# Third attention of a long two-block program: which PSUM banks hold scores and turned weights, and the order of TensorE's work in a step

## What is computed

```python
q = q.reshape(B, S, Hk, G, D) * (D ** -0.5)          # Hk=2 key/value heads, G=4 query heads each, D=64
...
s_c = einsum('bqhgd,bnhd->bhgqn', qc, kc) + head_bias(dist_c)      # compressed keys (31)
p_c = masked_softmax(s_c, dist_c >= 0)
...
s_s = einsum('bqhgd,bhqnkd->bhgqnk', qc, k_sel) + bias_s            # selected blocks of 64 keys
p_s = masked_softmax(s_s, mask_s)
...
s_w = einsum('bqhgd,bkhd->bhgqk', qc, kwc) + head_bias(dist_w)      # window of 512 keys
p_w = masked_softmax(s_w, mask_w)
...
return gc[..., 0:1] * o_c + gc[..., 1:2] * o_s + gc[..., 2:3] * o_w
```

## Time and profile before

| | us |
|---|---|
| median of 3 runs | 2223.79 (2222.8 to 2226.46) |
| the profiled execution, in all | 2226.47 |
| its span in the trace | 2224.7 |
| TensorE busy | 2183.1 (98%) |
| VectorE busy | 1276.9 (57%) |
| ScalarE busy | 945.7 (43%) |
| GpSimd busy | 804.4 (36%) |
| mean granted clock of TensorE | 0.994 |

### The profile page before, as it was taken

How to read it: one execution, slowest core, us unless ns; L and a number is a source line. 1 busy time by engine, 2 the same in 40 slices (tenths; PEclk the granted TensorE clock), 3 DMA queues, 4 the chain that set the end, 5 groups by cost and what they waited for, 6 DMA issues and landing times.

```text
span 2224.7 us, 25927 instructions
## 1 busy us (share of the span) xinstructions
PE 2183.1 (98%) x10008; PEld 1711.2 (77%) x10008; DVE 1276.9 (57%) x2198; ACT 945.7 (43%) x1558; POOL 804.4 (36%) x315
## 2 busy tenths in 40 slices
PE   8999999999999999999999999999999999999998
PEld 5777788888887767667888888887774688888887
DVE  6887665553258688773665562176967643333224
ACT  6676443333233566663344332233237532222224
POOL 1232444444443222113444444433330144444432
PEclk9999999999999999999999999999999999999999
DMA  8211333333222211112233333244310133233222
GB/s 281 67 58 53 93 95 98 102 95 104 95 93 78 72 48 39 39 33 90 96 99 95 95 105 103 90 125 165 112 60 11 38 95 95 95 99 109 91 100 85
DMA packets 58650, 199.97 MB, mean 90 GB/s; under 512 B 6720, under 2 KB 10320, under 8 KB 58528
## 3 DMA queue, kind: packets, MB, share of 16 engines
q1 hardware_dynamic: 57584, 196.21, 27.5%
q10 hardware_dynamic: 944, 2.11, 0.3%
HBM read 196.15 MB, written 7.38 MB: 91 GB/s over the span
## 4 chain that ended last, share of the span: by engine, by line
PE 88%; DVE 7%; ACT 2%; issue 1%; DMA 1%; POOL 0%; SPq 0%; DVEq 0%; ACTq 0%
PE lin L535 24%; PE lin L537 24%; PE lin L536 24%; PE obank L869 1%; PE scores L847 1%; PE turn L668 1%; PE scores L851 1%; PE stat L674 1%; PE scores L1070 1%; PE lin L586 1%; PE obank L748 1%; PE lin L588 1%; PE lin L587 1%; PE scores L705 1%; PE obank L1046 1%
## 5 line engine op out<-in xcount | busy, mean ns | idle before, releaser
L2540 POOL TENSOR_TENSOR w_lo<-slots,w_hi 128x1024 fp32r<-128x1024 f32 (+4 forms) x309 | 801.5, 2596 | 1395.9 <-ACT w_hi L2021 1395.9
L2021 ACT ACTIVATE w_hi<-slots 128x1024 fp32r<-128x1024 f32 (+4 forms) x312 | 347.0, 1113 | 576.9 <-DMA slots<-in_w_ffn_in 281.0
L535 PE MATMUL lin<-g_hi,w_hi 128*128 128x512 f32 x1400 | 550.0, 393 | 0.0
L537 PE MATMUL lin<-g_hi,w_lo 128*128 128x512 f32 x1400 | 545.0, 389 | 0.0
L536 PE MATMUL lin<-g_lo,w_hi 128*128 128x512 f32 x1400 | 544.9, 389 | 0.0
L535 PEld LDWEIGHTS lin<-g_hi,w_hi 128*128 128x128 f32 x1400 | 262.8, 188 | 59.3 <-issue 5.0
L536 PEld LDWEIGHTS lin<-g_lo,w_hi 128*128 128x128 f32 x1400 | 262.8, 188 | 55.8 <-issue 1.7
L537 PEld LDWEIGHTS lin<-g_hi,w_lo 128*128 128x128 f32 x1400 | 262.7, 188 | 54.7
L1255 DVE TENSOR_TENSOR h<-lin,h 128x512 f32<-128x512 f32 x72 | 49.7, 690 | 306.1 <-PE lin L537 296.9
L536 PE MATMUL lin<-f_lo,w_hi 128*128 128x512 f32 x528 | 205.4, 389 | 0.0
L535 PE MATMUL lin<-f_hi,w_hi 128*128 128x512 f32 x528 | 205.4, 389 | 0.0
(11 more groups left out here) (479 smaller groups left out, 3526.9 us busy)
## 6 DMA issues: line engine op xcount, KB each, us to landing
slots<-in_w_ffn_in SPq DMA_DIRECT2D x132, 512.0 KB, 3.5
slots<-in_w_ffn_out SPq DMA_DIRECT2D x48, 704.0 KB, 4.0
slots<-in_w_ple SPq DMA_DIRECT2D x24, 640.0 KB, 3.8
slots<-in_w_a_qkv SPq DMA_DIRECT2D x24, 512.0 KB, 3.6
slots<-in_w_c_in SPq DMA_DIRECT2D x21, 512.0 KB, 3.6
slots<-in_w_b_wo SPq DMA_DIRECT2D x16, 512.0 KB, 3.5
slots<-in_w_b_pair SPq DMA_DIRECT2D x8, 768.0 KB, 4.2
slots<-in_w_a_wo SPq DMA_DIRECT2D x16, 256.0 KB, 2.6
```

Source lines behind the costliest of these rows:

```text
L535: pe.matmul(bank[:, parity, :], hi, x_hi, start=k == 0, stop=False)
L537: mm = pe.matmul(bank[:, parity, :], lo, x_hi, start=False, stop=k == len(rhs) - 1)
L2021: ac.activation(w_hi[:, slot, at_], slots[:, slot, at_], ACT.Copy).then_inc(q.hi_made, 1)
L2540: po.tensor_tensor(w_lo[:, slot, at_], slots[:, slot, at_], w_hi[:, slot, at_].bitcast(F32), ALU.subtract).then_inc(q.weights_split, 1)
```

## The change

Three things change, all in this loop.

*Banks.* Scores get a second pair, `stat` and `lin[:, 1]`. A group is block 0, block 1, or blocks 2 and 3 together; groups alternate between the two pairs from group 2 on, and block 3 lies behind block 2 in the same bank. Turned weights have three banks left, `turn[:, 0]`, `turn[:, 1]` and `lin[:, 0]`, which rotate: block 0 takes banks 0 and 1 (x = 0, 1), block 1 takes 2 and 0, blocks 2 and 3 take 1 and 2.

*Order.* TensorE's step becomes: turn 0, score 0, turn 1, score 1, all four value products, turn 2 and 3, score 2 and 3.

*Waits.* They follow the banks. VectorE waits for both short blocks before it reads the first; ScalarE likewise before it copies. The first short scores wait for the logarithm that reads `stat`, and that `inv_sqrt` moves on ScalarE from the start of step 1 to before the exponentials of step 0's block 2.

```diff
-        turns = (turn, lin)
+        turned_banks = (turn[:, 0, :], turn[:, 1, :], lin[:, 0, :])
+        def turned_bank(k, x):
+            bank = turned_banks[(2 * min(k, 2) + x) % 3]
+            return bank[:, 2 * P:] if k == 3 else bank
+        def score_bank(n, x):
+            group, k = 3 * (n // NQ) + min(n % NQ, 2), n % NQ
+            bank = (stat[:, :], lin[:, 1, :])[x] if group >= 2 and group % 2 == 0 else scores[:, x, :]
+            return bank[:, 2 * P:] if k == 3 else bank
...
             def score(s, k):
                 i = NQ - 1 - k
-                wait(pe, q.c_biased, 8 * s + 2 * k)
+                n = 4 * s + k
+                if n == 2:
+                    pe.wait_ge(q.gl_log, 2)
+                    pe.wait_ge(q.tile_taken, TILE["c_in"] + len(C_IN))
+                elif k < 3:
+                    wait(pe, q.c_biased, 2 * n if n < 2 else 8 * s + (-4, 0, 2)[k])
...
-            for s in range(CH + 2):
-                for k in range(NQ):
-                    i = NQ - 1 - k
-                    if s == 1 and k == 0:
-                        pe.wait_ge(q.cc_copied, 2)
-                    if 0 < s <= CH:
-                        n = 4 * (s - 1) + k
+            def turned_weights(s, k):
+                if 0 < s <= CH:
+                        n, i = 4 * (s - 1) + k, NQ - 1 - k
                         pe.wait_ge(q.c_weights, 2 * n + 2)
                         for x in range(2):
-                            wait(pe, q.c_tcopied, 2 * n - 3 + x)
-                            turn_weights(sc(s - 1, i, x), i, turns[n % 2][:, x, :]).then_inc(q.c_turned, 1)
-                    if s < CH and 4 * s + k > 1:
-                        score(s, k)
-                    if s > 1:
-                        c_out_product(s - 2, k)
+                            if k < 3:
+                                wait(pe, q.c_tcopied, 8 * (s - 1) + ((-4, -1), (0, 1), (2, 3))[k][x])
+                            turn_weights(sc(s - 1, i, x), i, turned_bank(k, x)).then_inc(q.c_turned, 1)
...
+            for s in range(CH + 2):
+                if s == 1:
+                    pe.wait_ge(q.cc_copied, 2)
+                for ks in ((0,), (1,), (2, 3)):
+                    for k in ks:
+                        turned_weights(s, k)
+                    for k in ks:
+                        scored(s, k)
+                    if s > 1 and ks == (1,):
+                        for j in range(NQ):
+                            c_out_product(s - 2, j)
...
-                ve.wait_ge(q.c_scored, n + 1)
+                ve.wait_ge(q.c_scored, n + (2 if k == 2 else 1))
...
             for s in range(CH + 1):
-                if s == 1:
-                    inv_sqrt(gl_e[:, 1, :], GV, q.gl_ss, q.gl_log, q.gl_fac, 2, 2)
...
                     if s < CH and 4 * s + k > 1:
                         exps(s, k)
+                    if s == 0 and k == 1:
+                        inv_sqrt(gl_e[:, 1, :], GV, q.gl_ss, q.gl_log, q.gl_fac, 2, 2)
                     if s > 0:
                         for x in range(2):
-                            ac.wait_ge(q.c_turned, 8 * (s - 1) + 2 * k + x + 1)
+                            ac.wait_ge(q.c_turned, 8 * (s - 1) + 2 * (3 if k > 1 else k) + x + 1)
```

More of the change, by code:

```diff
@@ L1066, in score @@
                 i = NQ - 1 - k
-                wait(pe, q.c_biased, 8 * s + 2 * k)
+                n = 4 * s + k
[4 more added lines that the diff above has]
+                    wait(pe, q.c_biased, 2 * n if n < 2 else 8 * s + (-4, 0, 2)[k])
                 for kv in range(2):
                     rows = slice(64 * kv, 64 * kv + 64)
-                    mm = pe.matmul(scores[:, kv, 0:LEN[i]], c_z[rows, s // 2, i * P:(i + 1) * P],
+                    mm = pe.matmul(score_bank(n, kv)[:, 0:LEN[i]], c_z[rows, s // 2, i * P:(i + 1) * P],
                                    c_z[rows, 4 + s % 2, 0:LEN[i]], start=True, stop=True)
@@ L1112, in _, with scored @@
                     recurrence_sums(1)
-            for s in range(CH + 2):
-                for k in range(NQ):
-                    i = NQ - 1 - k
-                    if s == 1 and k == 0:
-                        pe.wait_ge(q.cc_copied, 2)
-                    if 0 < s <= CH:
-                        n = 4 * (s - 1) + k
+            def turned_weights(s, k):
+                if 0 < s <= CH:
+                        n, i = 4 * (s - 1) + k, NQ - 1 - k
                         pe.wait_ge(q.c_weights, 2 * n + 2)
                         for x in range(2):
-                            wait(pe, q.c_tcopied, 2 * n - 3 + x)
-                            turn_weights(sc(s - 1, i, x), i, turns[n % 2][:, x, :]).then_inc(q.c_turned, 1)
-                    if s < CH and 4 * s + k > 1:
-                        score(s, k)
-                    if s > 1:
-                        c_out_product(s - 2, k)
+                            if k < 3:
+                                wait(pe, q.c_tcopied, 8 * (s - 1) + ((-4, -1), (0, 1), (2, 3))[k][x])
+                            turn_weights(sc(s - 1, i, x), i, turned_bank(k, x)).then_inc(q.c_turned, 1)
+            def scored(s, k):
+                if s < CH and 4 * s + k > 1:
+                    score(s, k)
+            for s in range(CH + 2):
[9 more added lines that the diff above has]
+                            c_out_product(s - 2, j)
             output_products("c_out", DC + BH, list(zip(c_o_hi, c_o_lo)))
@@ L1913, in biased @@
                 n, i = 4 * s + k, NQ - 1 - k
-                ve.wait_ge(q.c_scored, n + 1)
+                ve.wait_ge(q.c_scored, n + (2 if k == 2 else 1))
                 wait(ve, q.c_turned, 2 * n - 6)
                 for x in range(2):
-                    ve.tensor_tensor_reduce(out=sc(s, i, x), in0=scores[:, x, 0:LEN[i]],
+                    ve.tensor_tensor_reduce(out=sc(s, i, x), in0=score_bank(n, x)[:, 0:LEN[i]],
                                             in1=c_bias[:, s // 2 + 4 * x, S - LEN[i]:S], scale=-(CD ** -0.5), scalar=3e38,
@@ L2476, in _ @@
                             ac.activation(c_pts[(s - 1) % 2][:, x, 0:i + 1, i * P:(i + 1) * P],
-                                          turns[k % 2][:, x, 0:LEN[i]].rearrange("p (j c) -> p j c", c=P), ACT.Copy)\
+                                          turned_bank(k, x)[:, 0:LEN[i]]
+                                          .rearrange("p (j c) -> p j c", c=P), ACT.Copy)\
                                 .then_inc(q.c_tcopied, 1)
```

## The result

The changed kernel takes 2277.4 us (median of 4 runs, 2268.0 to 2279.8) against 2223.3 us (median of 4 runs, 2221.5 to 2226.5), a ratio of 1.0234 with a 95% interval of 1.0202 to 1.0266. It is slower by 54 us; 2276 was forecast. The profiled execution is the fastest of the four, 2268.0, with a span of 2266.3 us, 41.6 us more than before's.

A forecast was written before the change was run, and what follows sets the result against it. TensorE was taken to bound the kernel, holding 88% of the chain that ended last. Waits +29.5 us and clock drops +23 gave +52 on the median 2223.8, so 2276, range 2250 to 2290.

The forecast's parts named there:

- TensorE's work: TensorE's own work per loop step: 7.72 us, 1.00 more with V (compressed part, every second step); average 8.2 against 9.15.
- Wait at T1: Before turning block 1's weights, TensorE waits for ScalarE's copy of block 0 of the same step: idles 2.6 us.
- Wait at T0: Turning block 0's weights, TensorE waits for ScalarE's copy of block 3 from the step before: idles 2.8 us.
- Start and end: Loop's start, up to step 3's first turn, 29.7 us against 24.0 (+5.7); its end 12.2 against 10.0 (+2.2).
- The sum with the full clock: Whole loop without clock drops: five full steps +21.6, start +5.7, end +2.2, together +29.5 us.
- The clock: Idle pieces close together in each loop step make TensorE's clock drop to half: +23 us taken, bounds 0 and +54.
- (1) The clock holds: Rival: TensorE's clock stays at full speed in the loop, only waits cost: +29.5 us, 2253; chance 0.22.
- (2) Low nearly throughout: Rival: TensorE's clock stays low nearly throughout the loop: +75 to +83 us, 2303; chance 0.08.
- (3) Faster: Rival: ScalarE's copies don't end the turns' waits; steps of 8.2 us, -7 us, 2217; chance 0.04.
- (4) Only one wait binds: Rival: one of the two turn waits binds; steps of 10.8 us, +10, 2234; chance 0.05 with what lies between.

The follow-up runs named there:

- e7: Changed kernel with ScalarE's copies and exponentials reordered to serve banks as TensorE needs them, next step's block 0 copy early: 2224.2 us, ratio 0.9994.
- e3: Changed kernel with only the copies of blocks 0 and 1 put before the same block's exponentials on ScalarE: 2241.4 us, ratio 1.0066.
- e2: Changed kernel with ScalarE's copies before the same block's exponentials, both short blocks' copies before both their exponentials: 2230.5 us, ratio 1.0028.
- e1: Changed kernel with TensorE repeating the first turn of blocks 0 and 1 five more times to fill its idle pieces: 2259.0 us, ratio 1.0145.
- e8: e7 with first short scores on the first bank pair and the last value products behind the last turns: 2218.8 us, ratio 0.9966 to the kernel before.
- e9: Changed kernel with the grouping of value products undone, each block's product again behind its own group's scores: 2259.1 us, ratio 1.0160.
- e4: Changed kernel with only the copies of blocks 2 and 3 put before those blocks' exponentials on ScalarE: 2263.3 us, ratio 1.0160.
- e5: Kernel before with only the four value products of a step put in a row after block 1's scores: 2233.7 us, ratio 1.0032.

## Why the prediction was right, point by point

**TensorE's work.** Foreseen 7.7 us a step, 8.7 with V. Shown by e7 without waits for copies: 8.10 and 8.70, the first with 0.23 to 0.24 at the output bank in it. The four products together take a row of 2.37 in the changed kernel's last step, at full clock, as the 2.38 (2.31 by starts) read from before's. In the changed kernel's timeline T2 and T3 together go from 1716.40 to 1717.20, 0.80, and S2 and S3 from there to 1718.06, 0.86, where 0.90 was taken between 0.85 and 1.05.

**Wait at T1.** Foreseen 2.6; measured 2.35 in the step that ran at full clock and 1.99 to 2.17 in the others from step 2 on, where some of the work beside it ran at half clock. For step 2 the prediction had 3.6 and 2.02 was measured, its largest miss of a wait. The circle itself took 3.96 against 4.04. e3 and e2 show its cause.

**Wait at T0.** Foreseen 2.8; measured 2.63 in six of seven steps. From S3's end at 1718.06 to T0's second half at 1721.35 are 3.29 us against 3.3 summed; the idle piece is shorter than 2.8 because T0's first half has a row of 0.66, where 0.50 was taken off.

**Start and end.** Foreseen 29.7 and 12.2 us at full clock; measured 33.7 (1668.5 to 1702.1) and 13.6 (1782.0 to 1795.5), both with halved clock in them. The wait for the logarithm was 1.7 against 2.0, those of step 1 were 4.75 and 1.76 against 5.0 and 2.3.

**The sum with the full clock.** +29.5; e1, with the clock nearly whole, has +30.9 in its loop, +28.4 without its own low stretch, and steps of 13.13 and 14.13 against 13.1 and 14.1.

**The clock.** The mechanism was right, the size of its term was not. The prediction's parts add up to a loop of 110.3 us (63.6 of work and 46.7 of waits) and it put +23 for the clock on it, 133.3 in all. The table has 64.9, 39.7 and 22.5, in all 127.1. The slowed work, 22.5, is as large as the +23, though in nine unequal stretches (1.7 to 5.4 us each) and not as one drop of 3.0 in each of eight steps. But the waits were 7.0 us shorter than summed: 3.3 at the start, half of it at T1 of step 2, 3.3 in the five full steps and 0.4 at the end. Of the 3.3 in the full steps about 1.2 are slowed work that ran inside T1's wait (1.99 to 2.17 against 2.35), the rest is that each piece was taken 0.17 to 0.25 too long; for the start the two causes are not told apart.

What the clock really cost is therefore less than its slowed work, 15.4 us by e1's loop and 18.4 by the medians, so the prediction's +23 was 5 to 8 us too large, and for the profiled execution its sum was 6 us too high. That the medians meet all the same (2277.4 and 2276) is partly luck: the other three executions are 7.5 to 11.8 us slower than the profiled one, and the prediction has no term for that.

The rule of the Trainium skill ("TensorE: Matmul & The Clock Gate", section "A second HAM failure mode: psum-queue depth-cycling") is that the clock swings where a kernel cycles through PSUM banks with small pauses between groups. The nine low stretches agree with it; but e2 and e8 cycle through as many banks with the clock at 0.94 and 0.93, so here it is the pauses that count, and e9 and e4 add that it depends on how they are cut.

**Rivals.** (1) The clock holds: it did not, nine stretches at 1.2 GHz; e1, where it nearly held, took 2259, against 2253 foreseen for this rival. (2) Low nearly throughout: no, TensorE was at 1.2 GHz for 58.0 of 127 us. In seven of the nine stretches it came back in the value products, within the unbroken work from T1 to T0, as the prediction's argument against this rival had it; but three stretches also began in that work (1696.7, 1727.4 and 1775.2). (3) Faster: the copies did end the waits. The condition given, the copy ahead of the exponentials on ScalarE, was tried: e2 is not yet faster than before, since T1's copy stands behind the short blocks' exponentials, e7 is even, and e8 is 7.1 us faster than the kernel before beside it (2225.9), as much as the rival had, though with the ends of the loop mended too. (4) Only one wait binds: both did; e3 and e4 take one each away.

## What to carry over

When banks are moved from one use to another, read the wait counts of the use that gets fewer, and for each ask which instruction of the reader's queue stands ahead of the awaited one: here a copy stood behind an exponential that needed scores that the waiting engine had not yet made or had only just made, and three idle engines were the result. The cure was not more banks but the reader's order, served as the writer needs them. Grouping matmuls saved 0.15 to 0.3 us for each switch here (value products 2.31 in place of 2.76 us for three switches, T2 and T3 0.80 in place of 1.08 for one), but the pieces that were drawn together had been the cover of another wait (e5).

## What the runs showed of the hardware that was not expected

Repeating TensorE work that nobody needs made the kernel 18 us faster (e1), since the clock went from 0.77 to 0.97 in the loop. And for nearly the same idle time (33.4 and 39.7 us), three pieces of 0.8 to 1.8 us a step left the mean clock at 0.89, two pieces of 2.0 to 2.6 with 2 us of work between brought it to 0.77; with 34.0 us, mainly in one piece of 3.4 to 4.4 a step, it was 0.82 (e4). Where exactly the clock falls within a step varied from step to step in the trace and stays open.
